# Splitting a block of 32x32 matmuls in a paged attention stage in two, with the orders of VectorE and ScalarE that follow

## The reference

```
# prompt: 16 heads of 64, query blocks of 128, causal, cum = running sum of the log forget gates
logits = q @ k.T * DH**-0.5 + cum_q - cum_k      # masked
o = softmax(logits) @ v
# samples: 8 sequences, 16 pages of 128 past rows each, plus 4 new rows
k_all = concat(k_pool[page_table], k); v_all = concat(v_pool[page_table], v)
logits = q @ k_all.T * DH**-0.5 + suffix_k - suffix_q   # masked
o = softmax(logits) @ v_all
```

## Time and profile before

| | |
|---|---|
| median of 3 runs | 3735.44 us |
| the profiled execution | 3732.01 us |
| its span, first to last instruction | 3730.4 us |
| PE busy | 3241.8 us (87%) |
| PE weight loads busy | 2943.6 us (79%) |
| DVE busy | 1602.6 us (43%) |
| ACT busy | 971.4 us (26%) |
| mean granted TensorE clock | 0.903 |
| HBM read | 348.68 MB |

### The profile page before, as it was taken

One profiled execution on the slowest core, in us unless ns is written; L12 is line 12 of the kernel. 1 busy time (PEld: TensorE's weight loads), 2 busy tenths in 40 slices (PEclk: granted clock), 3 DMA queues, 4 the chain that ended last, 5 costly groups with the idle time before them and its releaser, 6 DMA issues.

```text
span 3730.4 us, 65316 instructions
## 1 busy us (share of the span) xinstructions
PE 3241.8 (87%) x27579; PEld 2943.6 (79%) x27579; DVE 1602.6 (43%) x2086; ACT 971.4 (26%) x1423; POOL 244.7 (7%) x331
## 2 busy tenths in 40 slices
PE   7998899997977888869999854479999899889997
PEld 6897799997864444469999743479998798779997
DVE  2324544324224444354442399664432422464422
ACT  2301322223202233232222244332222310232222
POOL 0000000003300000000000078000000000000000
PEclk9996899998987888889999887689999898789998
DMA  3213223322337776632323110123232120322321
GB/s 95 57 34 102 74 86 88 91 74 65 89 105 269 303 297 257 236 94 85 90 86 89 45 45 23 40 63 89 86 89 63 57 79 23 113 68 87 91 86 47
DMA packets 466048, 369.42 MB, mean 99 GB/s; under 512 B 16777, under 2 KB 429886, under 8 KB 465884
## 3 DMA queue, kind: packets, MB, share of 16 engines
q1 hardware_dynamic: 449808, 348.72, 29.6%
q10 hardware_dynamic: 11980, 17.28, 1.4%
q0 software_dynamic: 4096, 1.06, 0.3%
HBM read 348.68 MB, written 17.26 MB: 98 GB/s over the span
## 4 chain that ended last, share of the span: by engine, by line
PE 81%; DVE 9%; issue 5%; ACT 3%; DMA 1%; ACTq 0%; DVEq 0%; SPq 0%
PE acc L716 55%; PE acc L697 6%; PE acc L1049 3%; DVE big L1297 3%; PE acc L1092 2%; PE acc L912 2%; PE acc L900 1%; DVE rstd L1327 1%; PE acc L1010 1%; PE acc L776 1%; PE acc L1001 1%; PE acc L985 1%; DVE yT L1361 1%; PE acc L1225 1%; PE acc L990 1%
## 5 line engine op out<-in xcount | busy, mean ns | idle before, releaser
L716 PE MATMUL acc<-h_hi,wsp 128*128 128x272 f32 x5632 | 944.0, 290 | 66.1 <-DVE h_lo L1583 66.1
L1319 DVE TENSOR_TENSOR wsp<-ring,wsp 128x1024 fp32r<-128x1024 f32 (+1 forms) x320 | 416.8, 1305 | 1169.1 <-ACT wsp L1880 1169.1
L716 PEld LDWEIGHTS acc<-h_hi,wsp 128*128 128x128 f32 x5632 | 798.6, 190 | 68.7 <-issue 68.4
L1880 ACT ACTIVATE wsp<-ring 128x1024 fp32r<-128x1024 f32 (+1 forms) x320 | 358.6, 1124 | 1303.2 <-PE acc L716 1294.1
L716 PE MATMUL acc<-h_lo,wsp 128*128 128x272 f32 x3328 | 690.2, 289 | 0.0
L716 PEld LDWEIGHTS acc<-h_lo,wsp 128*128 128x128 f32 x3328 | 527.2, 190 | 0.0
L716 PE MATMUL acc<-g_hi,wsp 128*128 128x272 f32 x2816 | 473.9, 290 | 24.0 <-DVE g_lo L1578 24.0
L716 PEld LDWEIGHTS acc<-g_hi,wsp 128*128 128x128 f32 x2816 | 401.3, 191 | 24.9 <-issue 24.9
L716 PE MATMUL acc<-i_hi,wsp 128*128 128x272 f32 x1536 | 265.6, 295 | 37.2 <-DVE i_lo L1347 32.4
L716 PE MATMUL acc<-g_lo,wsp 128*128 128x272 f32 x1408 | 292.7, 290 | 0.0
L716 PEld LDWEIGHTS acc<-i_hi,wsp 128*128 128x128 f32 x1536 | 225.0, 196 | 39.7 <-issue 35.6
(11 more groups left out here) (288 smaller groups left out, 3104.6 us busy)
## 6 DMA issues: line engine op xcount, KB each, us to landing
ring<-in_ffn_w SPq DMA_DIRECT2D x176, 512.0 KB, 3.8
mix<-in_cache_fox_k SPq DMA_DIRECT2D x128, 512.0 KB, 6.9
ring<-in_cache_fox_v SPq DMA_DIRECT2D x106, 512.0 KB, 6.9
ring<-in_ffn_w SPq DMA_DIRECT2D x64, 704.0 KB, 4.7
ring<-in_conv_w SPq DMA_DIRECT2D x24, 512.0 KB, 3.9
mix<-in_cache_fox_v SPq DMA_DIRECT2D x22, 512.0 KB, 6.6
ring<-in_gla_wr SPq DMA_DIRECT2D x16, 512.0 KB, 4.0
ring<-in_gla_wv SPq DMA_DIRECT2D x16, 512.0 KB, 4.1
```

The costliest lines, as they stand in the source:

```text
L716: last = pe.matmul(acc[:, bank + h, 0:HALF], wsp[:, s, w, k * P:(k + 1) * P], rhs[:, k0 + k, h * HALF:(h + 1) * HALF], start=start and k = ...
L1319: dve.tensor_tensor(wsp[:, s, 1, 0:tiles * P], ring[:, slot, 0:tiles * P], wsp[:, s, 0, 0:tiles * P], ALU.subtract).then_inc(wlo_done, 1)
L1880: act.activation(wsp[:, slot % SPLITS, 0, 0:tiles * P], ring[:, slot, 0:tiles * P], ACT.Copy)\
```

## The change

`sample_scores` is cut into three calls. The bias matmuls and the wait for the transposed pages are now `sample_bias(G)`; the 128 matmuls are issued as 64 for the first two heads of each row group and 64 for the last two, with the 32 for the new keys behind the second 64. Between the two halves stand `turn_output`, `scores_of_pair` and `weigh(v, 0)`. In every step `weigh(v, 1)` moves behind the first `turn_item`, `output` behind the second, and `weigh(v, 2)` and `weigh(v, 3)` stand together ahead of `values_of_pair`. The transpose of the new keys' weights (pn) leaves `turn` and goes to the head of `weigh(v, 0)`. No matmul, copy or transfer is added or taken away.

On DVE the sixth page of a group (page 5) now stands between the two row maxima of the pair in the odd step, and in the even step the pages and the maxima of z stand behind the maxima and reciprocals of the pair. The core of the diff:

```diff
-            def sample_scores(G):
+            def sample_bias(G):
...
                 pe.wait_ge(turned, KG * (G + 1))
-                for c in range(GH4):
+
+            def sample_scores(G, heads, new):
+
+                b, half = G // HALVES, G % HALVES
+                NK = KG * 32
+                for c in heads:
...
-                if half == HALVES - 1:
+                if new and half == HALVES - 1:
...
-                last.then_inc(ksc_full, 1)
+                return last
...
                 if u == 0:
                     pe.wait_ge(zexp_done, b + 1)
-                    pe.wait_ge(orow_done, b)
-                    pe.transpose(acc[0:NS, 5, 256:256 + P], z[:, KEYS:ZN], ident[:]).then_inc(pn_full, 1)
...
                 if u == 0 and g == 0:
+                    pe.wait_ge(orow_done, b)
+                    pe.transpose(acc[0:NS, 5, 256:256 + P], z[:, KEYS:ZN], ident[:]).then_inc(pn_full, 1)
+                if g == 0:
+                    pe.wait_ge(pt_out, v + 1)
+                if u == 0 and g == 0:
                     pe.wait_ge(pn_out, b + 1)
...
-                if g == 0:
-                    pe.wait_ge(pt_out, v + 1)
                 pe.wait_ge(v_in[n % V_SLOTS], 16 * (n // V_SLOTS + 1))
...
                     v, pair = s - LAG, s < PAIR_STEPS
                     if v >= 0:
                         turn(v)
-                    if s % 2 == 0 and 2 <= s <= 2 * DB * HALVES:
-                        sample_scores(s // 2 - 1)
+                    scored, G = s % 2 == 0 and 2 <= s <= 2 * DB * HALVES, s // 2 - 1
+                    if scored:
+                        sample_bias(G)
+                        sample_scores(G, (0, 1), False)
                     if 0 < s <= PAIR_STEPS:
                         turn_output(s - 1)
                     if pair:
                         scores_of_pair(s)
                     if v >= 0:
                         weigh(v, 0)
+                    if scored:
+                        sample_scores(G, (2, 3), True).then_inc(ksc_full, 1)
+                    if pair:
+                        turn_item(2 * s)
+                    if v >= 0:
                         weigh(v, 1)
                     if pair:
-                        turn_item(2 * s)
+                        turn_item(2 * s + 1)
                     if v > 0 and v % GR == 0:
                         output(v // GR - 1)
                     if v >= 0:
                         weigh(v, 2)
-                    if pair:
-                        turn_item(2 * s + 1)
-                    if v >= 0:
                         weigh(v, 3)
                     if pair:
                         values_of_pair(s)
...
-                    if more:
-                        turn_pages(G, (3, 4, 5) if s % 2 else (0,))
+                    if more and s % 2:
+                        turn_pages(G, (3, 4))
+                    if pair:
+                        for x in range(2):
+                            n = item(2 * s + x)[2]
+                            dve.wait_ge(sc_full, 2 * s + x + 1)
+                            dve.tensor_reduce(nmax[:, x:x + 1], acc[:, 6 + x, 0:n], AX.X, ALU.max, negate=True)\
+                               .then_inc(pmax_done, 1)
+                            if more and s % 2 and x == 0:
+                                turn_pages(G, (5,))
+                    if v > 0 and v % GR == 0:
+                        output(v // GR - 1)
+                    if more and s % 2:
+                        turn_pages(G, (6, 7))
+                    if pair:
+                        for x in range(2):
+                            dve.wait_ge(pexp_done, 2 * s + x + 1)
+                            dve.reciprocal(rsum[:, x:x + 1], rsum[:, x:x + 1]).then_inc(rinv_done, 1)
+                    if more and s % 2 == 0:
+                        turn_pages(G, (0,))
...
-                    if pair:
...
+                    if more and s % 2 == 0:
+                        turn_pages(G, (1, 2))
...
                     v, pair = s - LAG, s < PAIR_STEPS
                     if v >= 0:
-                        if v % GR == 0:
-                            act.wait_ge(pn_full, v // GR + 1)
-                            act.activation(p_new, acc[0:NS, 5, 256:256 + P], ACT.Copy).then_inc(pn_out, 1)
                         act.wait_ge(pt_full, v + 1)
                         if v >= 2:
                             act.wait_ge(v_used, GR * (v - 1))
                         act.activation(ptb[:, v % 2, :], acc[:, 4, :], ACT.Copy).then_inc(pt_out, 1)
+                    if 0 < s <= PAIR_STEPS:
+                        q, h, n = item(2 * s - 2)
+                        act.wait_ge(ob_full, s)
+                        act.activation(big[:, h // 2, q * P:(q + 1) * P], acc[:, 6, 0:P], ACT.Copy).then_inc(ob_out, 1)
+                    if v >= 0 and v % GR == 0:
+                        act.wait_ge(pn_full, v // GR + 1)
+                        act.activation(p_new, acc[0:NS, 5, 256:256 + P], ACT.Copy).then_inc(pn_out, 1)
...
+                            if half == HALVES - 1:
+                                act.wait_ge(pn_full, b)
                         if half == HALVES - 1:
...
-                    if 0 < s <= PAIR_STEPS:
...
+                    if pair:
+                        for x in range(2):
+                            n = item(2 * s + x)[2]
+                            act.wait_ge(tr_full, 2 * s + x + 1)
+                            act.activation(pT[:, x, 0:n], acc[:, 6 + x, 0:n], ACT.Copy).then_inc(tr_out, 1)
                     if scored and half == HALVES - 1:
                         act.wait_ge(nmx_done, b + 1)
```

More of the change, by code:

```diff
@@ L1033, in sample_scores @@
                 if half == HALVES - 1:
-                    new = slice(NK, NK + NS)
                     pe.matmul(acc[:, 1, NK + b * DS:NK + (b + 1) * DS], ident[:], upto4, start=False, stop=False,
                               skip_group_check=True)
-                    pe.matmul(acc[:, 1, new], pick[NS:2 * NS, b % 2].rearrange("p h i -> p (h i)"),
+                    pe.matmul(acc[:, 1, NK:NK + NS], pick[NS:2 * NS, b % 2].rearrange("p h i -> p (h i)"),
                               bias_nq[:, NS * B:NS * (B + 1)], start=False, stop=False, skip_group_check=True,
@@ L1049, in sample_scores @@
                                 last = pe.matmul(acc[32 * j:32 * (j + 1), a, 0:NK], qz[quad, h, f, :],
-                                                 kT[quad, :, at:at + 32], start=False, stop=(cell == 2 * GH4 - 1),
+                                                 kT[quad, :, at:at + 32], start=False, stop=(c == GH4 - 1 and f == 1),
                                                  skip_group_check=True, tile_position=(32 * a, 32 * j))
-                if half == HALVES - 1:
+                if new and half == HALVES - 1:
                     for c in range(GH4):
@@ L1056, in sample_scores @@
                                 h = GH4 * j + c
-                                last = pe.matmul(acc[32 * j:32 * (j + 1), 1, new], qz[NS:2 * NS, h, f, :],
+                                last = pe.matmul(acc[32 * j:32 * (j + 1), 1, NK:NK + NS], qz[NS:2 * NS, h, f, :],
                                                  k_rep[:, 2 * (c % 2) + f, h // 2, :], start=False,
@@ L2152, in fox @@
                         act.activation(ptb[:, v % 2, :], acc[:, 4, :], ACT.Copy).then_inc(pt_out, 1)
+                    if 0 < s <= PAIR_STEPS:
[8 more added lines that the diff above has]
+                            n = item(2 * s + x)[2]
+                            act.wait_ge(pmax_done, 2 * s + x + 1)
+                            act.activation(probs[x][:, 0:n], acc[:, 6 + x, 0:n], ACT.Exp, bias=nmax[:, x:x + 1],
+                                           accum_out=rsum[:, x:x + 1]).then_inc(pexp_done, 1)
                     scored = s % 2 == 0 and 2 <= s <= 2 * DB * HALVES
@@ L2166, in fox @@
                            .then_inc(ksc_out, 1)
-                    if 0 < s <= PAIR_STEPS:
-                        q, h, n = item(2 * s - 2)
-                        act.wait_ge(ob_full, s)
-                        act.activation(big[:, h // 2, q * P:(q + 1) * P], acc[:, 6, 0:P], ACT.Copy).then_inc(ob_out, 1)
+                    if pair:
+                        for x in range(2):
+                            n = item(2 * s + x)[2]
+                            act.wait_ge(tr_full, 2 * s + x + 1)
+                            act.activation(pT[:, x, 0:n], acc[:, 6 + x, 0:n], ACT.Copy).then_inc(tr_out, 1)
                     if scored and half == HALVES - 1:
@@ L2176, in fox @@
                     if pair:
-                        for x in range(2):
-                            n = item(2 * s + x)[2]
-                            act.wait_ge(pmax_done, 2 * s + x + 1)
-                            act.activation(probs[x][:, 0:n], acc[:, 6 + x, 0:n], ACT.Exp, bias=nmax[:, x:x + 1],
-                                           accum_out=rsum[:, x:x + 1]).then_inc(pexp_done, 1)
```

(4 more changed lines are left out.)

1 line of the change is left out of this document (removed).

## The result

| | before | after |
|---|---|---|
| median of 4 runs | 3736.18 us | 3689.51 us (3684.05 to 3699.96) |
| the profiled execution | 3732.01 us | 3686.43 us |
| its span | 3730.4 us | 3684.9 us |
| mean granted clock | 0.903 | 0.912 |

The ratio is 0.9877, with a 95% interval of 0.9853 to 0.9902: some 46 us faster, where 28 had been forecast. The measured time lies inside the range of 3680 to 3742 us, near its fast end.

The account below looks back on a forecast made before the run. PE, in its own order, was taken to bound the attention stage, stalling for 256-instruction blocks. Terms -22.5 - 6 + 17 + 8 - 22 = -25.5 us took 3732.0 to 3706.5 us profiled; forecast 3707, range 3680 to 3742 (8 in 10).

Parts of the forecast that it names:

- The stall (term 1): Samples' scores on PE: cutting the burst lets instruction blocks arrive in time; stalls fall from 38.6 to 16 us, gain 22.5.
- L985: PE's wait for ACT's copy, no longer behind the copies into z: 1.02 to 0.57 us in even steps, gain 6 us.
- The odd steps: Moved weigh, page 5 between the maxima and the later new-key transpose make PE wait: loss 17 us, bounds 8 to 22.
- The exponential of z: It comes late, once per sequence, and the next step's turn waits for it: loss 8 us, between 4 and 12.
- The clock: Attention stage of layer 1: less idle time behind bursts means less time at low clock; gain 22 us, bounds 0 to 47.
- kT: DVE's chain of pages to the next burst: its cover shrinks from 9 to 3.6 us and stays, cost 0.
- The rival of late pages: Pages of keys land late, delaying the next burst by 2.5 us in 15 groups: 37 us, to 3744 us; chance 0.13.

Follow-up runs that it names:

- the shift: 32 tiny matmuls (128 instructions) added on PE in step 0: to the changed kernel, 3686.22 us (0.9876); to the kernel before, 3745.45 us (1.0039).
- The kernel with the wait: Changed kernel plus a PE wait in even steps, behind the second half of the scores, until DVE has turned two pages of the next group: 3754.04 us, 1.0061.
- the copy alone: Kernel before with one edit, ACT's copy of turn_output ahead of the copies into z, the burst left whole: 3731.01 us, 0.9985.
- the kernel with two repairs: Changed kernel with weigh's order in odd steps restored and the new keys' transpose between turn_output and the pair's scores: 3686.26 us, 0.9862.

## Why the prediction was right, and where its sizes were off

1. The stall (term 1) was right in mechanism and in most places; the grid decided, as the shift shows. The size was too small: 30.6 us went, not 22.5. Group 5 had its full stall (3.55) and group 3 one of 2.71. Group 1 had none: the clock is low there, and a half takes 4.5 us instead of 2.8, so the block came in time. Group 7's stood where foretold, ahead of the second `turn_item`, but was 0.95 us and not 2.4 to 2.9; groups 10 and 12 had under 0.5. The prediction let a block arrive 5.1 to 6.2 us behind the boundary before it. At the 19 places named above it was 3.2 to 5.9 us, and before the change the longest stalls of groups 1, 8, 13 and 15 were 0.7 to 1.6 us, not 2.3 to 3.4.
2. L985: -9.3 instead of -6, since in the even steps the wait is 0.37, less than the odd step's 0.57 that I had taken.
3. The odd steps: 10.1 + 3.9 = 14 us instead of 17. The place and both waits were as worked out (0.56 and 0.48). What I missed is that the transpose's old place has a wait of its own now, 6.4 us.
4. The exponential of z: +5.8 instead of 8.
5. The clock is the term that was mis-sized most: 32 us, not 22. Its mechanism, idle time behind the burst, was only argued in the prediction. The kernel with the wait shows that such idle time lowers the clock; how much of the 32 us is due to the stalls that went isn't shown, since the copy alone had 5.2 us of it, and other kernels changed their clock at the same or at less idle time.
6. kT: the cover shrank and held. DVE waited 5.0 us for pages instead of 1.6, PE almost never for kT. The rival of late pages, the slower side, did not happen.

The five terms in 1 to 5 were all off to the same side, by 8, 3, 3, 2 and 10 us, so none of them hid another. Against these 27 us stand the 1.9 us of L1010 and 6 us outside the stage, which the prediction didn't have. That leaves the profiled execution, 3686.4 us, some 20 below the 3706.5 forecast for it. The prediction also has a slip: with the 3.4 us that it names the median would have been 3710, and not 3707.

## What to carry to other kernels

A wait that the trace calls "issue" and that ends a long row of small instructions should be measured in instructions, not in us: cut the windows in the middle of two stalls and count. If the counts are multiples of one number, look for packets of the queue of instructions at the same times; the cure is to put slower work between, not to take waits away. And read the engine's busy time beside its idle time, since the clock can double a gain or eat it: here 20.0 us less idle time came with 31.5 us less busy time, 41.7 us more with 26.8 more, and in the kernel with two repairs 9 to 10 us less with 17 to 18 more.

## What the runs showed of the hardware

In this stage PE's instructions come in blocks of 256, one packet of 16384 bytes each. Small matmuls use a block up in 2.8 us at the full clock, and the next is then up to 3.6 us late (3.55 us in group 5 of the changed kernel). Where slower work lies between, a block lasts up to 18.9 us (from 1142.8 to 1161.7 in the kernel before), and PE doesn't stand still. Adding 128 instructions where PE waited anyway moved stalls of 3 us in and out of bursts 100 us later, without any other change to the work.
